# Fused recurrence and projection stage: the inverse by products of (I+P) with [P-I, X] over two column quarters and two banks, with the projection products spread between the groups of small products

## Time and profile before

| | |
|---|---|
| median of 3 runs | 2325.97 us (2320.78 to 2330.53) |
| the profiled execution | 2317.24 us, its span 2315.7 us |
| mean granted TensorE clock | 0.984 |
| TensorE busy (matmul) | 2215.1 us, 96% |
| VectorE busy | 1032.3 us, 45% |
| ScalarE busy | 717.5 us, 31% |
| GpSimd busy | 407.9 us, 18% |

### The profile page before, as it was taken

The page is one execution under the profiler, slowest core; times in us unless marked ns, Lnnn a source line. Parts: engine busy times, 40 slices in busy tenths (PEclk is TensorE's granted clock), DMA queues, the critical chain, the costliest instruction groups (busy, mean ns, idle before and its releaser), DMA issues. The chain is left out here.

```text
span 2315.7 us, 64509 instructions
## 1 busy us (share of the span) xinstructions
PE 2215.1 (96%) x28004; PEld 1453.8 (63%) x28004; DVE 1032.3 (45%) x2221; ACT 717.5 (31%) x1446; POOL 407.9 (18%) x506
## 2 busy tenths in 40 slices
PE   7999999999999999999997999998999999999996
PEld 4444445445555555555556766756888888888884
DVE  3336767833654654644656765655211111111114
ACT  4224545623454543543642322222000000000003
POOL 1012222310000000000002120013524333233231
PEclk9999999999999999999998999998999999999998
DMA  4103444443333333333338754262999999999997
GB/s 144 37 23 128 153 147 137 167 113 93 94 105 88 91 103 94 94 104 89 84 107 258 233 169 132 97 236 70 363 381 335 357 364 328 354 357 335 353 335 293
DMA packets 359966, 436.66 MB, mean 189 GB/s; under 512 B 164994, under 2 KB 296198, under 8 KB 351536
## 3 DMA queue, kind: packets, MB, share of 16 engines
q1 hardware_dynamic: 343232, 397.94, 50.5%
q0 software_dynamic: 14384, 35.19, 6.0%
q10 hardware_dynamic: 2112, 0.01, 0.1%
HBM read 329.84 MB, written 104.50 MB: 188 GB/s over the span
## 5 line engine op out<-in xcount | busy, mean ns | idle before, releaser
L1202 PE MATMUL h_pp<-hT,r_wcol 128*128 128x512 f32 x832 | 414.0, 620 | 3.3 <-ACT h_iraw L1317 3.3
L2925 PEld LDWEIGHTS e_ps_gu<-e_xT,e_wu 128*128 128x128 f32 x2048 | 233.6, 192 | 14.3 <-issue 14.3
L2925 PE MATMUL e_ps_gu<-e_xT,e_wg 128*128 128x128 f32 x2048 | 235.2, 276 | 0.0
L2925 PE MATMUL e_ps_gu<-e_xT,e_wu 128*128 128x128 f32 x2048 | 233.8, 275 | 0.0
L2925 PEld LDWEIGHTS e_ps_gu<-e_xT,e_wg 128*128 128x128 f32 x2048 | 232.5, 193 | 0.4 <-DVE e_xT L3043 0.4
L2934 PE MATMUL e_ps_y<-e_wd,e_hid 128*128 128x512 f32 x512 | 225.1, 592 | 0.8 <-DVE e_hid L3097 0.8
L1202 PEld LDWEIGHTS h_pp<-hT,r_wcol 128*128 128x128 f32 x832 | 141.8, 190 | 124.6 <-issue 109.4
L522 PE MATMUL h_pp<-hT,r_wcol 128*128 128x512 f32 x480 | 209.1, 593 | 1.3 <-DVE hT L794 1.3
L3050 DVE TENSOR_SCALAR e_y<-e_ps_y,e_row 128x512 f32<-128x512 f32 x31 | 23.3, 750 | 325.0 <-PE e_ps_y L2934 325.0
L2934 PEld LDWEIGHTS e_ps_y<-e_wd,e_hid 128*128 128x128 f32 x512 | 94.8, 190 | 108.8 <-issue 107.1
L522 PEld LDWEIGHTS h_pp<-hT,r_wcol 128*128 128x128 f32 x480 | 90.3, 191 | 109.7 <-issue 108.1
(11 more groups left out here) (428 smaller groups left out, 3398.3 us busy)
## 6 DMA issues: line engine op xcount, KB each, us to landing
e_wg<-in_moe_w_gate_dram SPq DMA_DIRECT2D x32, 2048.0 KB
e_wu<-in_moe_w_up_dram SPq DMA_DIRECT2D x32, 2048.0 KB
e_wd<-in_moe_w_down_dram SPq DMA_DIRECT2D x32, 2048.0 KB
r_wcol<-in_w_in_dram SPq DMA_DIRECT2D x35, 512.0 KB, 4.7
ar<-r_ar SPq DMA_DIRECT2D x24, 512.0 KB, 2.7
kb<-r_kb SPq DMA_DIRECT2D x24, 512.0 KB, 2.8
m_ar<-ar SPq DMA_DIRECT2D x48, 256.0 KB, 4.7
m_kb<-kb SPq DMA_DIRECT2D x48, 256.0 KB, 3.5
```

What stands on the lines that cost most here:

```text
L1202: last = nc.tensor.matmul(pp[n % 2][:], wcol[(k + 2) % 3][:, c], self.hT[:, c, span(s)], start=c == 0, stop=c == KT - 1)
L2925: last = nc.tensor.matmul(ps[:, q * P:(q + 1) * P], w[u][:, c, q * P:(q + 1) * P], xT[u][:, c * P:(c + 1) * P], start=c == 0, stop=c == KT ...
```

## The change

- `power`: the first factor is now I+P in place of P, and the second [P-I, X] in place of [P, X]. One product then gives both P^2-I and (I+P)X, and VectorE has no addition to X. VectorE instead adds a constant (I after the first product, 2I after later ones) to P^2-I, which gives I+P^2. It writes that to a spare part of the same PSUM tile (S), copies the 64 columns [P^2-I, X] to SBUF (N), and transposes the spare part from PSUM. For i = 1, N is an addition of [-I, I]. I0 now works on [M, I] (64 columns instead of 32), and `X0` and the tile `xt` are gone.
- The results of systems j = 2 and 3 go to the neighbour column quarter and to a second PSUM bank. The order is j = 0, 2, 1, 3, so a group of 16 products uses 8 tiles of the array. The same goes for the first part of `right` and for `solve`. `ps_a` and `ps_b` are one tile of two banks, and for that I0, I4 and I1 have one wait more each.
- TensorE's order: `project` is called eight times in a step, with 1, 1, 1, 1, 1, 2, 1, 1 products (the first is nothing from step 16 on). I3 comes before `grow(c)`, and between `grow(c)` and I0 is one projection product instead of I3 and two.
- VectorE's order: `grow(4)` is now before `grown` and `state`; P0 stays behind them.
- GpSimd makes 12 constants of 32x32 instead of 4 at the start; ScalarE's unit evacuations are placed anew around the solution's.

```diff
-            dve_a = Marks(self.sem("m_dve_first"), "mask0 mask1 P0 X0 P1 turn1 X1 P2 turn2")
-            dve_b = Marks(self.sem("m_dve_last"), "X2 P3 turn3 X3 P4 turn4 X4")
+            dve_a = Marks(self.sem("m_dve_first"), "mask0 mask1 P0 S1 N1 turn1 S2 N2 turn2")
+            dve_b = Marks(self.sem("m_dve_last"), "S3 N3 turn3 S4 N4 turn4 X4")
...
                     def power(ps, u, i):
-                        for j in range(PAIRS):
-                            for q in quad:
-                                if i == 0:
-                                    last = nc.tensor.matmul(ps[q, j, 0:CH], pw[u][q, j], m0[q, j], start=True, stop=True)
-                                elif i < 4:
-                                    last = nc.tensor.matmul(ps[q, j, 0:2 * CH], pw[u][q, j], px[u][q, j], start=True,
-                                                            stop=True)
+                        for j in (0, 2, 1, 3):
+                            for q in range(P // CH):
+                                r, o = quad[q], quad[q ^ (j // 2)]
+                                if i < 4:
+                                    last = nc.tensor.matmul(ps[o, j, 0:2 * CH], pw[u][r, j], px[u][r, j] if i else m0[r, j],
+                                                            start=True, stop=True)
...
-                        project(it, 0, 3)
+                        project(it, 0, 1)
                         if has_b:
                             self.waits(eng, dve_a.at("turn2", b))
                             power(ps_b, b % 2, 2).then_inc(*pe_b.inc("I2"))
+                        project(it, 1, 2)
                         if has_c:
                             solve(c)
+                        project(it, 2, 3)
                         if has_a:
                             scores(a)
                         project(it, 3, 4)
-                        if has_c:
-                            grow(c)
                         if has_b:
                             self.waits(eng, dve_b.at("turn3", b))
                             power(ps_b, b % 2, 3).then_inc(*pe_b.inc("I3"))
-                        project(it, 4, 6)
+                        if has_c:
+                            grow(c)
+                        project(it, 4, 5)
                         if has_a:
-                            self.waits(eng, dve_a.at("P0", a))
+                            self.waits(eng, dve_a.at("P0", a), dve_b.at("turn4", b) if has_b else None)
                             power(ps_a, a % 2, 0).then_inc(*pe_a.inc("I0"))
-                        project(it, 6, 9)
+                        project(it, 5, 7)
                         if has_b:
-                            self.waits(eng, dve_b.at("turn4", b))
+                            self.waits(eng, dve_b.at("turn4", b), dve_a.at("turn1", a) if has_a else None)
                             power(ps_b, b % 2, 4).then_inc(*pe_b.inc("I4"))
+                        project(it, 7, 8)
                         if has_a:
-                            self.waits(eng, dve_a.at("turn1", a))
+                            self.waits(eng, dve_a.at("turn1", a), dve_b.at("X4", b) if has_b else None)
                             power(ps_a, a % 2, 1).then_inc(*pe_a.inc("I1"))
+                        project(it, 8, 9)
...
                     def grow(marks, ps, b, i):
 
                         u = b % 2
-                        if i > 1:
-                            nc.vector.tensor_tensor(px[u][:, :, CH:], px[u][:, :, CH:], ps[:, :, CH:2 * CH], ALU.add
-                                                    ).then_inc(*marks.inc(f"X{i - 1}"))
-                        nc.vector.tensor_copy(px[u][:, :, 0:CH], ps[:, :, 0:CH]).then_inc(*marks.inc(f"P{i}"))
-                        self.waits(eng, marks.at(f"P{i}", b))
-                        nc.vector.transpose(pw[u][:], px[u][:, :, 0:CH]).then_inc(*marks.inc(f"turn{i}"))
+                        each = lambda lo, n: eyes[:, lo * CH:(lo + n) * CH].unsqueeze(1).broadcast_to((P, PAIRS, n * CH))
+                        spare = ps[:, :, 2 * CH:3 * CH]
+                        nc.vector.tensor_tensor(spare, ps[:, :, 0:CH], each(1 if i == 1 else 2, 1), ALU.add
+                                                ).then_inc(*marks.inc(f"S{i}"))
+                        if i == 1:
+                            nc.vector.tensor_tensor(px[u][:], ps[:, :, 0:2 * CH], each(0, 2), ALU.add
+                                                    ).then_inc(*marks.inc(f"N{i}"))
+                        elif i < 4:
+                            nc.vector.tensor_copy(px[u][:], ps[:, :, 0:2 * CH]).then_inc(*marks.inc(f"N{i}"))
...
+                        self.waits(eng, marks.at(f"S{i}", b))
+                        nc.vector.transpose(pw[u][:], spare).then_inc(*marks.inc(f"turn{i}"))
...
+                        if has_b:
+                            self.waits(eng, pe_b.at("I3", b))
+                            grow(dve_b, ps_b, b, 4)
                         if has_c:
                             self.waits(eng, pe_c.at("MO", c))
...
                         if has_a:
                             self.waits(eng, act_a.at("m0", a))
-                            nc.vector.transpose(pw[a % 2][:], m0[:]).then_inc(*dve_a.inc("P0"))
...
-                        if has_b:
-                            self.waits(eng, pe_b.at("I3", b))
-                            grow(dve_b, ps_b, b, 4)
+                            nc.vector.transpose(pw[a % 2][:], m0[:, :, 0:CH]).then_inc(*dve_a.inc("P0"))
```

More of the change, by code:

```diff
@@ L946, in mix_rwkv_project_hgrn @@
             kbt = [sb(f"m_kbt{u}", [P, G, RH]) for u in range(RING)]
-            m0 = sb("m_m0", [P, PAIRS, CH])
+            m0 = sb("m_m0", [P, PAIRS, 2 * CH])
             pw = [sb(f"m_pw{u}", [P, PAIRS, CH]) for u in range(2)]
             px = [sb(f"m_px{u}", [P, PAIRS, 2 * CH]) for u in range(2)]
-            xt = [sb(f"m_xt{u}", [P, PAIRS, CH]) for u in range(2)]
             rs = sb("m_rs", [P, PAIRS, RH])
@@ L973, in mix_rwkv_project_hgrn @@
             ps_s = psum("s", [P, 2, M, P])
-            ps_a = psum("a", [P, PAIRS, P])
-            ps_b = psum("b", [P, PAIRS, P])
+            ps_p = psum("p", [P, PAIRS, 2 * P])
+            ps_a = ps_b = ps_p
             ps_x = psum("x", [P, 2, SPAN])
@@ L1069, in _ @@
                     for r in quad:
-                        nc.gpsimd.affine_select(out=eye[r], in_=eye[r], compare_op=ALU.not_equal, fill=1.0, base=0,
-                                                pattern=[[-1, CH]], channel_multiplier=1).then_inc(filled, 1)
+                        for part, value in enumerate((-1.0, 1.0, 2.0)):
+                            e = eyes[r, part * CH:(part + 1) * CH]
+                            nc.gpsimd.affine_select(out=e, in_=e, compare_op=ALU.not_equal, fill=value, base=0,
+                                                    pattern=[[-1, CH]], channel_multiplier=1).then_inc(filled, 1)
                         for d, sign in ((0, 1), (1, -1)):
@@ L1256, in solve @@
                         self.waits(eng, act_c.at("r", c), dve_b.at("X4", c))
-                        for j in range(PAIRS):
-                            for q in quad:
-                                nc.tensor.matmul(ps_ru[q, j % 2, j // 2], xt[c % 2][q, j], rs[q, j], start=True, stop=True)
+                        for j in (0, 2, 1, 3):
+                            for q in range(P // CH):
+                                r = quad[q ^ (j // 2)]
+                                nc.tensor.matmul(ps_ru[quad[q], j // 2, j % 2], px[c % 2][r, j, CH:], rs[r, j], start=True,
+                                                 stop=True)
                         for i, d, w, h in by_turn:
@@ L1369, in _ @@
                             self.waits(eng, pe_c.at("R", c))
-                            nc.scalar.activation(rs[:].rearrange("p (i w) v -> p w i v", w=2), ps_ru, ACT.Copy
+                            nc.scalar.activation(rs[:].rearrange("p (w i) v -> p w i v", w=2), ps_ru, ACT.Copy
                                                  ).then_inc(*act_c.inc("r"))
-                        for k, s, turned in done_in(it, 0, 3):
+                        for k, s, turned in done_in(it, 0, 2):
                             unit(k, s, turned)
@@ L1380, in _ @@
                             last.then_inc(*act_c.inc("u"))
+                        for k, s, turned in done_in(it, 2, 3):
+                            unit(k, s, turned)
                         if has_a:
@@ L1388, in _ @@
                                 d = q % 2
-                                last = nc.scalar.activation(m0[quad[q]], sm[a % RING][quad[q], d * PAIRS:(d + 1) * PAIRS, 0:CH],
-                                                            ACT.Copy)
+                                last = nc.scalar.activation(
+                                    m0[quad[q], :, 0:CH].rearrange("p (w i) n -> p w i n", w=2),
```

(9 more changed lines are left out.)

19 lines of the change are left out of this document (9 added, 10 removed).

## The result

| | before | changed |
|---|---|---|
| median of 4 runs | 2325.61 us (2320.78 to 2330.53) | 2358.93 us (2348.64 to 2364.46) |
| ratio, 95% interval | | 1.0153 (1.0129 to 1.0178) |
| profiled execution / span | 2317.24 / 2315.7 us | 2348.64 / 2346.9 us |
| mean granted clock | 0.984 | 0.986 |
| mean step | 14.90 us | 15.50 us |

The changed kernel is 1.5% slower: 33 us by the medians, 31 us between the two profiled executions. The forecast was +20 us. Nearly all of the time lies in the fused stage. Its mean step is read as the earlier trace rows was, from the first and last start of the state's products (L1273 now): (1244.1 - 515.6) / 47 = 15.50 us, and 48 x 0.60 = 29 us of the 31.

The account below looks back on a forecast made before the run. TensorE's instruction order was taken to bound the fused stage. Terms 0 + 37 - 17 + 1 = +21, less 1 for covered gaps, gave +20 us: 2346 us as a median, range 2319 to 2376 with rivals.

Parts of the forecast that it names:

- The late P0: TensorE before I0: waits 0.80 us in each of 46 steps for VectorE's P0; 37 us, bounds 28 to 46.
- Tiles: TensorE's small groups: on eight tiles instead of four, six groups cost 0.38 us each and I4 0.35.
- Rival 3: Small groups keep the four-tile price: up to +58 us and fewer supply gaps, 2404 us, half of it 2375; chance 0.15.
- Blocks: TensorE's projection: seven smaller blocks instead of four, 0.86 us a product plus 0.20 a block; with faster groups, nothing net.
- Instruction supply: TensorE in the fused stage: wider-spaced groups remove two thirds of 25 us of late-packet gaps; -17 us, bounds 0 and -25.
- the P0 wait covers gaps (-1): TensorE before I0: some waits for P0 cover a supply gap, taking 1 us off the sum.
- VectorE, ScalarE, GpSimd: Other engines' changed work: VectorE and GpSimd cost nothing, ScalarE +1 us with bounds 0 and 8.
- what would show it: Signs in the timeline after: I0 idles 0.8 us, groups 0.38, one-product blocks 1.06, issue gaps about 8, step 15.3 us.

Follow-up runs that it names:

- four-tile kernels: Changed kernel with small-product results back in their own column quarter, so four tiles: 2397.26 us; the same with P0 made before `grown` and `state`: 2361.47 us.
- six blocks: Changed kernel with P0 made before `grown` and `state`, projection products in six blocks (2, 1, 1, 1, 2, 1 from step 16 on): 2317.75 us.
- five blocks: Changed kernel with P0 made before `grown` and `state`, projection products in five blocks (3, 2, 1, 1, 1 from step 16 on): 2326.05 us.
- tile pair: Two kernels, both the changed one with P0 made before `grown` and `state`, differing only in tiles: four tiles 2361.5 us, eight tiles 2321.2 us.
- without value loads: Value loads left out after the first two chunks: in the kernel before 2304.37 us, in the five-block kernel 2308.90 us.
- four tiles, P0 first: Changed kernel with small groups on four tiles instead of eight and VectorE making P0 before `grown` and `state`: 2361.47 us.
- P0 first: Changed kernel with one VectorE instruction moved, P0 made before `grown` and `state` instead of behind them: 2321.22 us.

## Why the direction was right and the size too small

**The late P0: right, the size 6 us over.** The prediction gave I0 a start 1.86 us after MO's group. The trace has 1.84, within 0.01, in all but one of the 46 steps. In 40 steps TensorE stood 0.78 (forecast 0.80). In the six others a turned unit lies in that gap (as 4 passes of L1211), so the wait hides its 0.43 us. The list has 31 us; the forecast was 37, its bounds 28 to 46. Taking the wait away gave 38 us by the medians and 29 by the profiled executions.

**Tiles: right.** 0.38 a group, where the forecast had 0.38 against bounds of 0.28 and 0.58; I4 0.28 (854.68 to 854.97) against 0.35. Rival 3 (the four-tile price stays) is refuted by the timeline after, and the four-tile kernels measure what it would have cost: 40 us. 32 passes in 0.38 us (857.46 to 857.84) are 12 ns each.

**Blocks: right.** A block of one product is 1.06 us, one of two 1.91 (852.77 to 854.68), as forecast. The clean step is 13.92. What the faster groups win goes into the three more blocks, each 1.06 in place of the 0.86 that a further product costs in a longer block. What the 0.20 between them is made of no run shows.

**Instruction supply: this step failed.** The prediction said "I take two thirds of the 25 us as gone, -17". They went from 23 to 22 (without the wait for ScalarE from 20 to 22). With -1 in its place the prediction's sum would have been +36, and with the measured 31 for P0 too it is +30, against 31 measured between the profiled executions.

The runs show what was wrong with it. The term counted the spacing of the groups and left out that the groups themselves became faster. With four tiles and the new spacing the gaps are 7.5 us, so spacing alone took away 15, which is close to the -17. With eight tiles, same spacing, they are 25, 23 of them supply: the cheaper groups gave it back. A group of 64 instructions that passes in 0.38 instead of 0.58 us uses up the instruction stream half as fast again, and, as I read the gaps, TensorE runs out between packets. The prediction compared the lengths of its closest runs of four groups, 1.68 us before and 2.58 after, with a projection block counted into the second. Without that block three groups stand together after, 192 loads and passes in 1.17 us (857.46 to 858.63), 164 a microsecond; before it was 256 in 1.68, 152 a microsecond. The stream was used no more slowly than before, only for shorter. Five and six blocks are the other side of the same: groups closer again, 38 and 33 us (33 and 29 without the wait for ScalarE). That the stream's use is what empties it fits these counts, but no run shows the stream itself.

Whether the P0 wait covers gaps (-1) can't be told: without it the gaps are 3.6 us more with eight tiles (2.1 of them the wait for ScalarE) and 3.2 fewer with four.

**What a gap is.** Of the gaps in the list under "issue", without the waits for ScalarE, 25 of 25 before, 17 of 18 after and 29 of 30 in five blocks end 1.2 to 1.6 us after an instruction packet (queue q8) has landed; the two others end 1.7 us after one. The three waits for ScalarE in five blocks do not fit this: they end 5.1, 0.4 and 4.7 us after one. The longest gap of after:

```profile
1076.02 0.44 PE L1222 MATMUL m_ps_s<-m_ar,m_kb 64*64 64x128 f32 x6
1078.60 1.08 PE L1222 MATMUL m_ps_s<-m_ar,m_kb 64*64 64x128 f32 x26 [2.14 <-issue]
```

Between 1076.0 and 1077.3 the DMA view has one instruction packet beside the data (packets, MB, share of the 16 engines over that stretch); by its record it started at 1076.03, as the group's first pass went, and landed at 1077.21, 1.39 us before TensorE went on.

```profile
q1 hardware_dynamic: 646, 0.45, 106.7%
q8 instruction: 1, 0.02, 5.7%
```

I read it as a packet that starts too late for the passes left, with some 2.6 us from its start to the next pass. The gaps grow with how fast the groups go by, 7.5 us at 0.58 a group and 25.2 at 0.38 in the tile pair, and something in the data traffic adds to them: without value loads they fell by 8 us in both kernels. The records show where the two coincide. Take the 1.5 us that end 1.3 us before TensorE goes on, and ask whether the 16 DMA engines are over 60% busy there, as in some 27% of the stage. So it is in 15 of 18 supply gaps after, in all 8 of "four tiles, P0 first", in 18 of 25 before and in 13 of 21 of "P0 first", but in 15 of 30 with five blocks and 9 of 27 with six. With groups spread apart, the gaps lay mostly where data crowded the engines, as in the rows above; with groups close together, half or more lay elsewhere. That is a coincidence in time, and no run moved the large transfers to test it. What in the value loads makes the gaps longer is open. Fewer packets in the other loads changed nothing, and doubling the loads ran into another limit.

**VectorE, ScalarE, GpSimd: right, nothing.** L1452, L1458, L1455 and L1462 take 0.30, 0.41, 0.41 and 0.31 us, also out of and into PSUM, and TensorE waits for none of them. No wait for ScalarE appears in the list after (forecast +1).

Against "what would show it": the wait at I0 came as said; groups 0.38, blocks 1.06 as said; the gaps did not fall to 8; the step rose to 15.50, not 15.3, and the 0.2 x 48 = 10 us between the two is the supply term less the smaller P0 (16 less 6).

## What to carry to other kernels

When an order is changed, hold the whole chain from a producer to its consumer through every other engine's queue (here MO's end, two other VectorE instructions, P0: 1.84 us) against what is left between them on the waiting engine: one instruction moved ahead was worth 38 us by the medians (29 by the profiled executions), and nothing else in the change could be told from zero. Faster small groups paid less here than their price says: of 61 us, 40 arrived, and some 16 of the rest went into supply gaps. And where a list of waits names no releaser, look at the other engines' records: a load that started 0.07 us after an evacuation's end, each time, was read here as a wait for it.

## What the runs showed of the hardware

- Supply gaps of 0.1 to 2.3 us, 8 to 33 us in a stage of some 730 (the column "gaps" less the wait for ScalarE): 8 with groups of 0.58, 23 with groups of 0.38 in the same places, 29 and 33 with these closer together in six and five blocks. In the five-block kernel they took some 10 of the 19 us that two blocks fewer should have won.
- The granted clock fell to 0.50 at some stops of about 2 us. In the five-block kernel TensorE stood 2.31 us, waiting for ScalarE at L1246, up to 630.74. The granted clock was 1.00 up to 630.00, 0.50 from 630.30 to 636.00 and 1.00 again from 637.00. Four projection products in it took 6.08 us from start to start of the groups, where 0.86 a product and 0.20 make 3.6. In the windows PEclk is the last but two, 0.93, 0.51 and 1.00:

```profile
630.28 0.36 ACT L1412 ACTIVATE m_oacc<-m_ps_x 128x256 f32<-128x256 f32 x1
630.71 0.47 PEld L1246 LDWEIGHTS m_ps_x<-m_v,m_sm 32*32 32x32 f32 x31 [2.44 <-issue]
```
```profile
630.74 0.68 PE L1246 MATMUL m_ps_x<-m_v,m_sm 32*32 32x64 f32 x32 [2.31 <-issue]
631.35 0.68 PE L1250 MATMUL m_ps_x<-m_state,m_ar 64*32 64x64 f32 x32
631.96 6.15 PE L1203 MATMUL h_pp<-hT,r_wcol 128*128 128x512 f32 x8
```
```profile
625.00:631.00 6.00, 3.62 (x124) 1.75 (x131) 4.14 (x11) 5.97 (x10) 0.00 (x0) 0.93 0.10 22
631.00:637.00 6.00, 6.00 (x70) 2.80 (x54) 3.24 (x7) 0.50 (x2) 0.00 (x0) 0.51 0.94 262
637.00:643.00 6.00, 6.00 (x195) 3.46 (x197) 4.17 (x12) 2.53 (x8) 0.00 (x0) 1.00 0.25 94
```

  The gap of 2.1 us in the changed kernel (at 1076) was followed by full clock (1.00 in 1076 to 1082 and after), and so was one of 2.31 with six blocks (at 671.5; 1.00 from 671 to 678), while the version without L1277 fell to 0.50 (547 to 550) after one of 1.86 (at 544.6). So a gap's length alone does not decide it. What does is open.
- With the value loads doubled SyncE issued most of them 0.64 us apart (816.10 to 825.02, fourteen). At that pace sixteen a chunk are 10.2 us of a step of some 14.9, an estimate; the sixteen of the step shown took 11.58 (813.44 to 825.02). The kernel was 75 us slower for them.
